# Two parts of the input in one matmul: 30 feature-major panels of a three-layer block

## The reference

```python
h = rms_norm(x, norm_g)
(qa, ka, va, ga, ub, vb, gb, qc, gc, ma, mb, mc) = split_cols(h @ w_in, IN_SPLITS)
out_a = moba_attention(rope(qa), rope(ka), va) * silu(ga)
out_b = gmlp_spatial_gate(ub, vb, ...) * silu(gb)
out_c = memory_cross_attention(qc, mem_n, w_mem_kv) * silu(gc)
y = sigmoid(ma) * (out_a @ w_a) + sigmoid(mb) * (out_b @ w_b) + sigmoid(mc) * (out_c @ w_c)
x = x + y @ w_out
```

## Time and profile before

| | |
|---|---|
| median of 3 runs | 1079.03 us (1078.39 to 1080.5) |
| profiled execution | 1080.45 us, span 1078.6 us, granted TensorE clock 0.984 |
| TensorE matmul busy | 1010.6 us (94%), 7760 matmuls |
| DVE busy | 708.5 us (66%) |
| ACT busy | 589.2 us (55%) |
| GpSimd busy | 135.9 us (13%) |
| chain that ended last | PE 73%, ACT 10%, DVE 9% |

### The profile page before, as it was taken

How to read it: one execution, slowest core, us unless ns; L and a number is a source line. 1 busy time by engine, 2 the same in 40 slices (tenths; PEclk the granted TensorE clock), 3 DMA queues, 4 the chain that set the end, 5 groups by cost and what they waited for, 6 DMA issues and landing times.

```text
span 1078.6 us, 18793 instructions
## 1 busy us (share of the span) xinstructions
PE 1010.6 (94%) x7760; PEld 970.6 (90%) x7760; DVE 708.5 (66%) x1021; ACT 589.2 (55%) x908; POOL 135.9 (13%) x124
## 2 busy tenths in 40 slices
PE   6989789999999999679999999999999999999996
PEld 6989779999988799569999998888999999999996
DVE  5886666788874565864888884556655557755664
ACT  6745636656653375675666653376564655434432
POOL 4012411243320000000133330000100000000000
PEclk9989999999999999799999999999999999999999
DMA  9552214887655536403866646636645443655541
GB/s 315 174 187 80 78 40 123 218 255 199 191 180 195 176 118 196 117 2 79 224 181 192 196 156 221 228 101 193 206 142 157 156 146 104 194 186 194 183 150 40
DMA packets 188149, 174.54 MB, mean 162 GB/s; under 512 B 4062, under 2 KB 177616, under 8 KB 188064
## 3 DMA queue, kind: packets, MB, share of 16 engines
q1 hardware_dynamic: 185872, 167.92, 49.9%
q0 software_dynamic: 2160, 5.41, 1.5%
q10 hardware_dynamic: 32, 0.01, 0.0%
HBM read 172.25 MB, written 1.07 MB: 161 GB/s over the span
## 4 chain that ended last, share of the span: by engine, by line
PE 73%; ACT 10%; DVE 9%; issue 4%; DMA 2%; POOL 1%; SPq 0%; ACTq 0%; POOLq 0%; DVEq 0%
PE bank L758 36%; PE bank L742 17%; PE bank L776 12%; PE bank L792 4%; ACT w_hi L1092 3%; DMA w_raw<-in_ab_w_in 2%; DVE w_lo L1396 2%; PE bank L822 1%; ACT le L1188 1%; ACT cc L1217 1%; DVE le_s L1724 1%; ACT le_s L1320 1%; POOL sp__80 L613 1%; ACT L1188 0%; PE bank L833 0%
## 5 line engine op out<-in xcount | busy, mean ns | idle before, releaser
L1396 DVE TENSOR_TENSOR w_lo<-w_raw,w_hi 128x2048 fp32r<-128x2048 f32 x157 | 358.7, 2289 | 192.1 <-ACT w_hi L1092 192.0
L1092 ACT ACTIVATE w_hi<-w_raw 128x2048 fp32r<-128x2048 f32 x157 | 299.9, 1915 | 257.6 <-PE bank L758 154.4
L758 PE MATMUL bank<-y_hi,w_hi 128*128 128x256 f32 x736 | 206.8, 281 | 4.7 <-DVE y_lo L1404 4.2
L758 PE MATMUL bank<-y_hi,w_lo 128*128 128x256 f32 x736 | 205.5, 279 | 0.0
L758 PE MATMUL bank<-y_lo,w_hi 128*128 128x256 f32 x736 | 205.2, 279 | 0.0
L742 PE MATMUL bank<-w_hi,x_hi 128*128 128x256 f32 x608 | 177.5, 292 | 11.3 <-DVE x_lo L1404 4.7
L742 PE MATMUL bank<-w_lo,x_hi 128*128 128x256 f32 x608 | 173.7, 286 | 0.0
L742 PE MATMUL bank<-w_hi,x_lo 128*128 128x256 f32 x608 | 173.6, 285 | 0.0
L758 PE MATMUL bank<-x_hi,w_hi 128*128 128x256 f32 x528 | 150.8, 286 | 0.0
L758 PE MATMUL bank<-x_lo,w_hi 128*128 128x256 f32 x528 | 149.5, 283 | 0.0
L758 PE MATMUL bank<-x_hi,w_lo 128*128 128x256 f32 x528 | 149.5, 283 | 0.0
(11 more groups left out here) (339 smaller groups left out, 1589.8 us busy)
## 6 DMA issues: line engine op xcount, KB each, us to landing
w_raw<-in_ffn_up SPq DMA_DIRECT2D x88, 512.0 KB, 5.2
w_raw<-in_w_in SPq DMA_DIRECT2D x37, 1024.0 KB, 5.3
w_raw<-in_ffn_down SPq DMA_DIRECT2D x22, 1024.0 KB, 5.0
w_raw<-in_ab_w_in SPq DMA_DIRECT2D x14, 1024.0 KB, 5.3
w_raw<-in_ple_gate SPq DMA_DIRECT2D x8, 1024.0 KB, 5.2
w_raw<-in_c_w_in SPq DMA_DIRECT2D x6, 1024.0 KB, 5.0
w_raw<-in_ab_w_out SPq DMA_DIRECT2D x4, 1024.0 KB, 5.2
w_raw<-in_c_w_out SPq DMA_DIRECT2D x4, 1024.0 KB, 5.3
```

What stands on the lines that cost most here:

```text
L758: mm = pe.matmul(bank[b][:, c * 256:c * 256 + 256], wv[w][:, k, c * P:(c + 1) * P], x[:, k, :], start=(k == 0 and m == 0), stop=(k == KT - ...
L1092: act.activation(whi[n % RING][:, :], raw[n % RAW][:, :], ACT.Copy).then_inc(*mark("weights_hi", ("hi", n)))
L1396: dve.tensor_tensor(wlo[n % RING][:, :], raw[n % RAW][:, :], plain(whi[n % RING][:, :]), ALU.subtract).then_inc(*mark("weights_lo", ("lo", ...
```

## The change

In the 30 F panels of fb, qb, qa, ka, qc, gc, ga, gb2, mc, mb and ma (F panels of up, mk and ub stay as they were), x_hi and x_lo lie side by side per contraction tile in one tensor x_both, and w_hi meets both in one matmul of 512 columns, which fills a bank: w_hi x_hi in its first half, w_hi x_lo in its second. w_lo x_hi is added into the first half with 256 columns. Each chunk now has a bank of its own, `pair(n, c)`: 4 + 2 (n mod 2) + c. At eviction ACT copies the second half of each bank to the destination, DVE adds the first half to it, and after both adds multiplies in SBUF by the row. A bank is released by the second add of its panel. In the first panel of a stage the two chunks alternate within k.

```diff
+BOTH = ("fb", "qb", "qa", "ka", "qc", "gc", "ga", "gb2", "mc", "mb", "ma")
-        XH, XL = (fixed(n, [P, KT, T], F32R) for n in ("x_hi", "x_lo"))
+        XB = fixed("x_both", [P, KT, 2, T], F32R)
+        XH, XL = XB[:, :, 0, :], XB[:, :, 1, :]
+        def pair(n, c):
+            return 4 + 2 * (n % 2) + c
@@ tensor, panel(n)
+                elif stage in BOTH:
+                    for c in range(2):
+                        claim(pair(n, c), ("summed_parts", n))
+                    wv = [w[:, :].rearrange("p (k n) -> p k n", k=KT) for w in (wh, wl)]
+                    first = i == 0
+                    for c, k in [(c, k) for k in range(KT) for c in range(2)] if first else [(c, k) for c in range(2) for k in range(KT)]:
...
+                        out = bank[pair(n, c)]
+                        pe.matmul(out[:, :], wv[0][:, k, c * P:(c + 1) * P], XB[:, k, :, :].rearrange("p a t -> p (a t)"),
+                                  start=k == 0, stop=False, skip_group_check=True)
+                        mm = pe.matmul(out[:, 0:T], wv[1][:, k, c * P:(c + 1) * P], XB[:, k, 0, :],
+                                       start=False, stop=k == KT - 1, skip_group_check=True)
+                        if k == KT - 1 and c == 0:
+                            mm.then_inc(*mark("product", ("chunk0", n)))
@@ scalar, panel(n), ahead of split(n + RING)
+                if stage in BOTH:
...
+                    for c in range(2):
+                        act.wait_ge(*at(("pe", n) if c else ("chunk0", n)))
+                        act.activation(dst[:, 2 * i + c, :], two(pair(n, c))[:, 1, :], ACT.Copy).then_inc(*mark("low_parts", ("low_part", n, c)))
@@ vector, panel(n)
-                    dve.wait_ge(*at(("pe", n)))
+                    if stage not in BOTH:
+                        dve.wait_ge(*at(("pe", n)))
...
+                    if stage in BOTH:
...
+                        for c in range(2):
+                            dve.wait_ge(*at(("low_part", n, c)))
+                            dve.tensor_tensor(dst[:, 2 * i + c, :], two(pair(n, c))[:, 0, :], dst[:, 2 * i + c, :], ALU.add).then_inc(*mark("parts_summed", ("summed_parts", n)))
+                        dve.wait_ge(*at(("summed_parts", n)))
...
+                            dve.tensor_tensor(dst[:, c2, :], dst[:, c2, :], row, ALU.mult).then_inc(*mark("scaled", event))
```

More of the change, by code:

```diff
@@ L746, in panel @@
                         return
+                elif stage in BOTH:
[4 more added lines that the diff above has]
+                    for c, k in [(c, k) for k in range(KT) for c in range(2)] if first else [(c, k) for c in range(2) for k in range(KT)]:
+                        if c == 0 and first:
+                            input_ready(k)
+                        if c == 0 and k == 2 and n - 1 in ROWS_AFTER:
+                            norm_row(ROWS_AFTER[n - 1])
+                        out = bank[pair(n, c)]
[5 more added lines that the diff above has]
+                            mm.then_inc(*mark("product", ("chunk0", n)))
                 elif kind == "F":
@@ L1123, in panel @@
                 ev = ("ev", n)
+                if stage in BOTH:
+                    dst = {"qa": qaT, "qb": qf, "fb": bdec, "ka": kaT, "qc": qc, "gc": gc, "ga": ga, "gb2": ubs, "mc": msig[0], "mb": msig[1], "ma": msig[0]}[stage]
+                    if stage == "ga" and i == 0:
+                        act.wait_ge(*at(("tr", "rope", 5)))
+                    if stage == "ma" and i == 0:
+                        act.wait_ge(*at(("yb", "c", 3)))
+                    for c in range(2):
+                        act.wait_ge(*at(("pe", n) if c else ("chunk0", n)))
+                        act.activation(dst[:, 2 * i + c, :], two(pair(n, c))[:, 1, :], ACT.Copy).then_inc(*mark("low_parts", ("low_part", n, c)))
                 if kind != "T" and not splits_later(n):
@@ L1526, in panel @@
                     row = row2(NORM_OF[stage])
-                    if stage == "qa":
-                        dve.scalar_tensor_tensor(qaT[:, c2, :], two(b), SB_DIM ** -0.5, row, ALU.mult, ALU.mult).then_inc(*mark("scaled", ev))
+                    if stage in BOTH:
+                        dst = {"qa": qaT, "qb": qf, "fb": bdec, "ka": kaT, "qc": qc, "gc": gc, "ga": ga, "gb2": ubs, "mc": msig[0], "mb": msig[1], "ma": msig[0]}[stage]
+                        for c in range(2):
+                            dve.wait_ge(*at(("low_part", n, c)))
+                            dve.tensor_tensor(dst[:, 2 * i + c, :], two(pair(n, c))[:, 0, :], dst[:, 2 * i + c, :], ALU.add).then_inc(*mark("parts_summed", ("summed_parts", n)))
+                        dve.wait_ge(*at(("summed_parts", n)))
+                        event = ev if stage in ("qa", "ka", "qc") else ("scaled", n)
+                        if stage == "qa":
+                            dve.scalar_tensor_tensor(qaT[:, c2, :], qaT[:, c2, :], SB_DIM ** -0.5, row, ALU.mult, ALU.mult).then_inc(*mark("scaled", event))
+                        else:
+                            dve.tensor_tensor(dst[:, c2, :], dst[:, c2, :], row, ALU.mult).then_inc(*mark("scaled", event))
                     elif stage == "ub":
@@ L1534, in panel @@
                     else:
-                        dst = {"qb": qf, "fb": bdec, "ka": kaT, "qc": qc, "gc": gc, "ga": ga, "gb2": ubs, "mc": msig[0], "mb": msig[1], "ma": msig[0]}[stage]
-                        event = ev if stage in ("ka", "qc") else ("scaled", n)
-                        dve.tensor_tensor(dst[:, c2, :], two(b), row, ALU.mult).then_inc(*mark("scaled", event))
+                        raise AssertionError(stage)
                 elif stage.startswith("gate"):
@@ L1663, in _ @@
                         fl = lambda x: x.rearrange("p a b -> p (a b)")
-                        dve.scalar_tensor_tensor(fl(XL[:, 4 + 2 * j:6 + 2 * j, :]), bank[2 + j][:, :], vec("hg_out_norm", 0)(0), plain(fl(XH[:, 4 + 2 * j:6 + 2 * j, :])), ALU.mult, ALU.subtract).then_inc(*mark("input_lo", ("xl", "hg", j)))
+                        dve.scalar_tensor_tensor(XL[:, 4 + 2 * j:6 + 2 * j, :], two(2 + j), vec("hg_out_norm", 0)(0), plain(XH[:, 4 + 2 * j:6 + 2 * j, :]), ALU.mult, ALU.subtract).then_inc(*mark("input_lo", ("xl", "hg", j)))
                 elif kind == "sb_weights":
```

## The result

The changed kernel takes 1092.53 us (median of 4 runs, 1091.51 to 1094.69) against 1079.66 (4 runs): ratio 1.0123, 95% interval 1.0104 to 1.0142, 1.0% to 1.4% slower. Forecast were 1090.9 and a range of 1082 to 1097. Its profiled execution took 1091.51 us (span 1089.6), 11.1 more than that of before.

What follows compares the result with a forecast made beforehand. TensorE was busy 94% of the span, but DVE's sum was taken to bound the first block. First block 6.0, attention 0.3, ub0 8.1, m panels -2.5: +11.9 us on 1079.03, so 1090.9 us; range 1082 to 1097.

Steps and rivals of the forecast that it cites:

- Merging: In every changed panel, one 512-column matmul replacing two of 256 saves 13.2 ns a pair, 6.3 us in 30 panels.
- m panels: Twelve panels of mc, mb and ma save 0.21 us each, 2.5 us, with their banks free in time.
- Adds and wait: On DVE, two adds and the scaling's wait cost 0.78 us per panel, bounded by 0.66 and 0.9.
- fb: In the first block's two fb panels, added work makes the second sigmoid start about 0.5 us later.
- The pause before qa0: TensorE waits 3.7 us for qb0's banks; the lower clock afterwards costs 0.8 us, bounds 0 and 1.5.
- First block: The first eight panels end 6.0 us later: 5.2 from added DVE work and fb, 0.8 from the clock after TensorE's pause.
- Attention: Second block, qc to ga: longer softmax waits (0.72) less qc's saving (0.42), +0.3 us, bounds -1.4 and +1.2.
- The wait before ub0: ub0 waits for gb2's third panel's bank: 5.7 us, plus 2.4 for the lower clock, +8.1, bounds 5.7 and 8.9.
- (a): Rival, 5%: adds and copies run in idle time everywhere and banks come free first; -6.3 us, 1072.7 us.
- (b): Rival, 14%: only the wait at ub0 counts, later slack returns the first block's 6.0 us; +5.9 us, 1084.9 us.
- (c): Rival, 10%: the first block counts, but ub0 does not wait and gb2 saves 0.6; +3.2 us, 1082.2 us.
- (d): Rival, 7%: merging does not save a matmul's fixed cost; +3.4 us on top of the forecast, 1094.3 us.

Runs made afterwards that it cites:

- grouped: Changed kernel with eight 512-column matmuls, then eight of 256, per chunk instead of alternating, except in a stage's first panel: 1092.0 us, ratio 1.0099 to the kernel before.
- fill_pause: Changed kernel plus 48 unused 256-column matmuls ahead of ub0's claim of its bank: 1091.49 us, ratio 1.0105 to the kernel before.
- m_only: Kernel before with merged matmuls only in the twelve panels of mc, mb and ma, no bank moved: 1079.05 us, ratio 0.9977.

## Why the prediction was right

The forecast was +11.9 us; +12.9 was measured between the medians and +11.1 between the profiled executions. The mechanism is the one that was forecast: DVE's adds in the first block, and one bank that a neighbour now holds, with the clock behind that wait. By its steps:

- **Merging** was mis-sized: 13.2 ns a pair from the down panels' 226.8 ns, 6.3 us in 30 panels. Measured are 23.04 against 22.61 us in mb and ma, 6.7 ns a pair, and 13.3 (23.04 against 22.19) in mc alone. The down panels' rate does not carry over: even among its own kind a 512-column matmul takes 230 ns in these stages. (226.8 - 213.3 is also 13.5 and not 13.3.) The isolated gap that the Trainium skill gives ("TensorE: Matmul & The Clock Gate", Back-to-back issue gap), by which a merge saves 2.5 ns, is too little for all three stages. m panels: -2.5 said, -1.7 measured.
- **Adds and wait, 0.78 us a panel:** 0.78 or 0.79 measured, six times, in full.
- **fb, +0.5:** it was about nothing. Counted from ACT's first w_hi (13.04 us, before 13.29) the second sigmoid starts after 15.82 us and started after 15.79 before; that it starts at 28.86 and not 29.08 is the earlier beginning of this execution. The two copies take 0.63 us together, not the 0.82 of the evictions with a scale. fb0's two copies (20.47) fitted in before its rows came (22.80), and before the change ACT waited 1.39 us for a weight panel ahead of its w_hi at 26.74, which now covers the rest.
- **The pause before qa0:** 3.7 us said, 3.64 from the last matmul's start to the next; its consequence 0.8 said, 0.2 measured, in the trace and by the run that removes it. First block: 6.0 said, 5.0 at ib's eviction when both executions are counted from that first w_hi (4.75 as they stand).
- **Attention, +0.3:** +0.1. The softmax waits grew by 1.0 us in all (L827 from 2.0 to 2.8, now L850; L1015 from 0.7 to 0.9, now L1038), much as said.
- **The wait before ub0:** 5.7 said, 5.5; **its clock** 2.4 said, 2.1 in this profile, and 1.3 to 2.4 over the six profiles that keep the pause. The run with other banks gives both back. The upper bound of this place is 5.7 + 2.7 = 8.4 by its own rows, not 8.9.

Terms that were too high (first block 1.7 at its end, ub 0.5, attention 0.2) and one too favourable (m, 0.8) offset each other in part, and 0.7 us in the store had no term at all. That the total came within 1 us is therefore partly luck. Of the rivals, (a) falls with the adds' 0.79 us, (b) with the run that restores the first eight panels, (c) with the pause of 6 us, (d) with the run of separate matmuls, though half of what it said holds in mb and ma; its +3.4 is 14 x 0.21 + 3 x 0.2 = 3.5.

## What to carry to other kernels

Fewer instructions of a bound engine are worth only what each saves where that engine ends last: here 7 to 13 ns each on 192 of 480 pairs, against 0.8 us of DVE per panel where DVE ends last. When a panel begins to hold two banks of four, go through every claim, also those of panels that were not changed. The price is set by how late the engine that reads the bank is (here DVE, which does layer_norm first: 5.5 us), and it has a second part, the clock after the pause (1.3 to 2.4 us). Apply such a change stage by stage; the same edit was a gain in twelve panels and a loss in the first eight.

## What the runs showed of the hardware that was not expected

- Merged matmuls that alternate with those of 256 columns run at one rate in mc (a panel in 5.55 us) and another in mb and ma (5.65), in every run that has them, with the same code and the granted clock at 1.00 in all. In the grouped order both take 5.59, and unmerged ones take 5.76 in all three. Why the alternating order differs by stage is open; it was not tried.
- The 1002 matmuls of up1 took 118.0 us in four profiles (before, changed, fill_pause, m_only) and 120.2 in the other nine, with the same code, at the same granted clock of 1.00. That is 2.2 us, a fifth of this change, and a reason to compare stages by their own length in the trace and not by where they stand.
- After nearly the same pause (5.5 to 6.0 us idle) the same 144 matmuls of ub took 18.75 to 19.88 us, against 17.4 without it.
- ACT evicts two 128x256 halves by a plain copy in 0.64 us (36.78) and with a per-partition scale in 0.82 us (76.17), 0.09 us more for each. The Trainium skill ("ScalarE: Activation LUTs", What ACT_TABLE_LOAD costs) states some 93 ns for such an operand; the two rows agree.
